# A two-block sequence model on one core: gate sigmoids placed ahead of other ScalarE steps, three output units run chunk by chunk, norm sums and one Toeplitz table product moved

## What is computed

```python
# odd mixer: 12 heads of 128 channels
p = h @ w_in                        # 1024 -> 1536 (xr) and 1536 (gate); h is RMS-normed
xc = causal_depthwise_conv(xr, conv_w, conv_b)       # 4 taps
r = sigmoid(xh @ w_rg + b_rg);  i = sigmoid(xh @ w_ig + b_ig)   # per head, 128x128 each
log_a = -8 * r * softplus(-lam);  a = exp(log_a)
bterm = sqrt(-expm1(2*log_a)) * (i * xc)
hs = associative_scan(a, bterm)     # along the sequence
h = h + (hs * silu(gate)) @ w_out
# block two, first mixer: a complex state space model, 64 groups of 16 channels, 64 states,
# then g = gelu(y + d*u), and out = (g @ w)[:, :1024] * sigmoid((g @ w)[:, 1024:])
```

## Time and profile before

| | us |
|---|---|
| median of 3 runs | 1717.25 |
| lowest and highest | 1715.61, 1717.97 |
| the profiled execution, its own time | 1717.2 |
| its span, first to last instruction | 1715.1 |
| PE busy | 1691.4 (99% of the span) |
| DVE, ACT, POOL busy | 871.1, 763.2, 967.1 |

### The profile page before, as it was taken

One profiled execution on the slowest core, in us unless ns is written; L12 is line 12 of the kernel. 1 busy time (PEld: TensorE's weight loads), 2 busy tenths in 40 slices (PEclk: granted clock), 3 DMA queues, 4 the chain that ended last, 5 costly groups with the idle time before them and its releaser, 6 DMA issues.

```text
span 1715.1 us, 20931 instructions
## 1 busy us (share of the span) xinstructions
PE 1691.4 (99%) x8044; PEld 1396.4 (81%) x8044; DVE 871.1 (51%) x1251; ACT 763.2 (44%) x1203; POOL 967.1 (56%) x606
## 2 busy tenths in 40 slices
PE   9999999999999999999999999999999999999998
PEld 7888888777778997888888888888678888888887
DVE  4999997757787885522212121386644221212124
ACT  5223335377867763343222222454765332323234
POOL 5859655657678575654444444664547444444464
PEclk9999999999999999999999999999999999999999
DMA  5322323222245233222222222222112222222221
GB/s 177 100 97 87 123 98 112 98 73 87 86 183 201 68 124 130 99 96 92 95 98 98 99 98 99 86 98 99 50 48 89 98 99 98 99 92 94 97 99 62
DMA packets 56258, 172.65 MB, mean 101 GB/s; under 512 B 6496, under 2 KB 14816, under 8 KB 55264
## 3 DMA queue, kind: packets, MB, share of 16 engines
q1 hardware_dynamic: 56160, 171.33, 28.9%
HBM read 165.01 MB, written 6.29 MB: 100 GB/s over the span
## 4 chain that ended last, share of the span: by engine, by line
PE 70%; DVE 5%; ACT 3%; issue 2%; POOL 1%; DMA 1%; SPq 0%; DVEq 0%; ACTq 0%
PE B L319 57%; PE B L1712 1%; PE B L2464 1%; PE B L2466 1%; PE B L2462 1%; PE B L2260 1%; PE B L2360 1%; PE B L2339 1%; DVE SW L1175 1%; PE B L302 1%; DVE B L1041 1%; PE B L1639 1%; PE B L1604 1%; PE B L304 1%; PE B L303 1%
## 5 line engine op out<-in xcount | busy, mean ns | idle before, releaser
L295 POOL TENSOR_TENSOR WL<-RAW,WH 128x1024 fp32r<-128x1024 f32 x280 | 679.0, 2427 | 618.3 <-ACT WH L291 618.0
L291 ACT ACTIVATE WH<-RAW 128x1024 fp32r<-128x1024 f32 x281 | 296.8, 1058 | 634.3 <-PE B L319 600.2
L319 PE MATMUL B<-P0h,WH 128*128 128x512 f32 x1088 | 424.6, 390 | 2.0 <-DVE Yl L444 1.8
L319 PE MATMUL B<-P0l,WH 128*128 128x512 f32 x1088 | 418.0, 389 | 0.3 <-DVE P0l L448 0.3
L319 PE MATMUL B<-P0h,WL 128*128 128x512 f32 x1088 | 274.4, 389 | 0.0
L319 PEld LDWEIGHTS B<-P0h,WH 128*128 128x128 f32 x1088 | 204.3, 188 | 45.8 <-DVE Yl L444 2.6
L319 PEld LDWEIGHTS B<-P0l,WH 128*128 128x128 f32 x1088 | 204.3, 188 | 42.8 <-DVE P0l L448 0.8
L319 PEld LDWEIGHTS B<-P0h,WL 128*128 128x128 f32 x1088 | 204.2, 188 | 42.4
L455 DVE TENSOR_TENSOR H<-H,B 128x512 f32<-128x512 f32 x88 | 60.2, 686 | 288.2 <-PE B L319 288.1
L1992 DVE SCALAR_TENSOR_TENSOR TMP<-B,RS 128x512 f32<-128x512 f32 x64 | 44.1, 691 | 258.5 <-PE B L319 244.1
L319 PE MATMUL B<-P1h,WH 128*128 128x512 f32 x448 | 174.7, 390 | 0.0
(11 more groups left out here) (362 smaller groups left out, 2686.5 us busy)
## 6 DMA issues: line engine op xcount, KB each, us to landing
RAW<-in_w SPq DMA_DIRECT2D x281, 512.0 KB, 3.2
PX<-in_zeros SPq DMA_DIRECT2D x4, 1024.0 KB, 9.4
H<-in_xT SPq DMA_DIRECT2D x8, 256.0 KB, 5.4
U<-u SPq DMA_DIRECT2D x32, 64.0 KB, 2.0
g<-GB SPq DMA_DIRECT2D x8, 256.0 KB, 2.2
GB<-g SPq DMA_DIRECT2D x32, 64.0 KB, 2.0
out<-Q SPq DMA_DIRECT2D x4, 512.0 KB, 3.6
CA<-in_zeros SPq DMA_DIRECT2D x1, 1920.0 KB, 10.0
```

The lines of the kernel that those rows point to most:

```text
L291: act.activation(WH[:, i % NS, :], RAW[:, i % NR, :], ACT.Copy).then_inc(*inc("w_hi", i))
L295: eng.tensor_tensor(WL[:, i % NS, :], RAW[:, i % NR, :], WH[:, i % NS, :].bitcast(F32), ALU.subtract).then_inc(*inc(lo_of(i), i))
L319: return pe.matmul(b[:, :], w[:, ws[c]], x[:, c, :], start=start, stop=stop)
```

## The change

In the odd mixer, ACT's work in slot X10 is only the weight copy; the first tap of X10 and the high part of X9 go into slot R1, between the sigmoids of heads 4 and 5 and those of heads 6 and 7, and the first tap of X11 and the high part of X10 behind the sigmoids of head 7. DVE's low part of X9 goes behind the scaling of X11. The one-column sigmoid stands after X8 in place of X9. The norm sums go from behind X0 into X1, behind its second chunk. In the state space stage, the table product of step 2 goes from behind `pe_v(2)` to ahead of `pe_y(0)`. The three output units run chunks 3 to 7 with the chunk outside and the unit inside.

```diff
             if kind in "XG":
-                linear(pe, what, P0h, P0l, range(8), ("x_lo", ("xc" if kind == "X" else "y", c)), "odd" if n == 0 else None)
+                linear(pe, what, P0h, P0l, range(8), ("x_lo", ("xc" if kind == "X" else "y", c)), "odd" if n == 0 else None,
+                       {1: lambda: stat_sums(pe, "odd", pool=rbanks)} if n == 1 else {})
...
-            if (kind, c) == ("X", 0):
-                stat_sums(pe, "odd", pool=rbanks)
-            elif (kind, c) == ("X", 1):
+            if (kind, c) == ("X", 1):
                 stat_spread(pe, "odd", pool=rbanks)
...
+    def held(n):
+
+        return 0 <= n < len(ODD) - 2 and ODD[n + 2] == ("R", 1)
...
-            if kind == "R":
+            if held(n):
+                highs(act, IDX[what] + 4)
+            elif kind == "R":
                 act_gates(act, pair(c, 0))
-                act_parts(act, n - 1)
-                if kind_at(n - 1) == "X":
+                if held(n - 2):
+                    act_first(act, n - 2)
+                    act_parts(act, n - 2)
+                else:
+                    act_parts(act, n - 1)
+                    if kind_at(n - 1) == "X":
+                        act_first(act, n - 1)
+                act_gates(act, pair(c, 1))
+                if held(n - 2):
                     act_first(act, n - 1)
-                act_gates(act, pair(c, 1))
-                if kind_at(n - 1) == "G":
+                    act_parts(act, n - 1)
+                elif kind_at(n - 1) == "G":
                     act_first(act, n - 1)
                 highs(act, IDX[what] + 3)
                 act_parts(act, n)
...
-            elif kind_at(n + 1) != "R":
+            elif kind_at(n + 1) != "R" and not held(n):
                 act_parts(act, n)
...
-            elif (kind, c) in (("X", 2), ("X", 9), ("G", 5)):
+            elif (kind, c) in (("X", 2), ("X", 8), ("G", 5)):
...
                     scaled(dve, XP[:, h % 2, 3:], ("in_odd", 0, h), "odd").then_inc(*inc("xp", h))
+                dve_parts(dve, n - 1, held(n - 1))
...
-            for unit, h in parted(n):
-                split_lo(dve, "xc" if unit == "X" else "y", h, Yl[:, h, :], own_bank(unit, h), Yh[:, h, :])
+            dve_parts(dve, n, not held(n))
...
+    def dve_parts(dve, n, due):
+        for unit, h in parted(n) if due else []:
+            split_lo(dve, "xc" if unit == "X" else "y", h, Yl[:, h, :], own_bank(unit, h), Yh[:, h, :])
...
         pe_transposes(pe, 3)
+        pe_toeplitz(pe, 2)
         for q in range(8):
             if q == 7:
                 banks.queue.extend(vbanks.queue)
-                pe_glu_start(pe, range(3))
+                pe_glu_start(pe)
             pe_y(pe, q)
             if q + 2 < 8:
                 pe_v(pe, q + 2)
-                pe_toeplitz(pe, q + 2)
+                if q:
+                    pe_toeplitz(pe, q + 2)
             if q + 4 < 8:
                 pe_transposes(pe, q + 4)
-        pe_glu_start(pe, range(3, 7))
         banks.queue.extend(ybanks.queue)
...
+    def pe_glu_start(pe):
 
         for what in GLU[:3]:
+            _, before = banks.take(what, "evac_a" if what[2] > 7 else "evac_d")
+            pe.wait_ge(*at(*before))
+            pe.wait_ge(*at("w_lo", IDX[what]))
+            for c in range(3):
+                pe_glu_chunk(pe, what, c)
+
+    def pe_glu_chunk(pe, what, c):
+
+        wh, wl = weights(IDX[what])
+        pe.wait_ge(*at("g_lo7" if c == 7 else "g_lo", ("g", c)))
+        ws = slice(128 * c, 128 * c + 128)
+        last = mm3(pe, banks.bank[what][:, :], wh[:, ws], wl[:, ws], P0h[:, c, :], P0l[:, c, :], c == 0, c == 7)
+        if c == 7:
+            last.then_inc(*inc("unit", what))
 
     def pe_glu(pe):
-        pe_glu_start(pe, range(7, 8))
+        for c in range(3, 8):
+            for what in GLU[:3]:
+                pe_glu_chunk(pe, what, c)
```

More of the change, by code:

```diff
@@ L1827, in program @@
     GLU = [("glu", 0, n + 8 * (1 - g)) for n in range(8) for g in range(2)]
-    def pe_glu_start(pe, chunks):
+    def pe_glu_start(pe):
         for what in GLU[:3]:
[L1832 to L1844, removed]
+            _, before = banks.take(what, "evac_a" if what[2] > 7 else "evac_d")
[10 more added lines that the diff above has]
+            last.then_inc(*inc("unit", what))
     def pe_glu(pe):
-        pe_glu_start(pe, range(7, 8))
+        for c in range(3, 8):
+            for what in GLU[:3]:
+                pe_glu_chunk(pe, what, c)
         for what in GLU[3:]:
```

## The result

The changed kernel takes **1722.67 us**, median of 9 runs (1720.76 to 1723.40), against 1717.25 (1715.61 to 1720.01) for the kernel before, 9 runs too: slower by 5.4 us by the medians. The ratio of all runs is 1.0027 [1.0019, 1.0036], or 4.6 us with an interval of 3.3 to 6.2, so the difference is clear of noise, but its size is known only to about 1.5 us. Forecast were 1721.9, range 1718.6 to 1724.3. The profiled execution took 1722.67 us with a span of 1720.6, where the kernel before had 1715.1, so the two traces differ by 5.5 us.

What follows compares the result with a forecast made beforehand. PE was taken as the bound, busy 99% of the span at full clock. On 1717.2 us, -0.9 + 0.6 + 5.1 + 2.5 - 2.6 = +4.7 gave 1721.9, range 1718.6 to 1724.3.

Steps and rivals of the forecast that it cites:

- norm sums: Sums moved behind two chunks of X1: the matmuls ahead fill 0.71 us of PE idle time; gain 0.9 us.
- gate steps: Odd mixer: R1 2.03 us shorter, but late taps delay y0's low part, G4 and G10; net loss 0.6 us.
- wait for the bank: Ahead of y(0): moved product waits for the copy of table product 1 until 582.7; loss 5.1 us.
- low clock: After the 6.9 us idle stretch, product and y(0) start at half clock; loss 2.5 us, bounds 1.7 to 4.4.
- output units: First three output units, chunk outside: the wait at chunk 6 goes; gain 2.6 us, bounds 2.3 to 2.7.
- Rival (c): Moved product's bank is free by 576, no wait, clock stays full: 1713.9, or 1711.3 with R1's gain; chance 0.05.
- Rival (a): Clock does not fall in the wait ahead of the product, all else as forecast: 1719.4 us; chance 0.12.
- rival (d): Low clock lasts 8.8 us, or the taps' chain passes on all its delay: 1723.8 to 1724.7; chance 0.09.
- Rival (b): Chain behind X9 to X11 has slack, so R1's gain of 2.0 us arrives: 1719.3 us; chance 0.12.

Runs made afterwards that it cites:

- third experiment: Kernel before with only the reordered gate steps of heads 4 to 7 and X9 to X11; 1717.82 us, ratio 1.0004.
- ninth experiment: Changed kernel with finer gate order and two-column sums spread in eights, table product of step 2 still ahead of y(0); 1717.73 us, ratio 0.9999.
- tenth experiment: Same kernel as the ninth experiment, plus 29 matmuls of 128x128 with unused results in the wait ahead of the table product; 1715.58 us, ratio 0.9991.
- the free bank: Changed kernel with the heads of two bank rings swapped, so the moved table product takes v(0)'s bank; 1715.14 us, ratio 0.9985.
- seventh experiment: Changed kernel with the table product back behind v(2) and sigmoids, high parts and first taps alternating more finely; 1712.35 us, ratio 0.9965.
- first experiment: Changed kernel with the table product of step 2 back behind v(2), all else kept; 1714.73 us, ratio 0.9988.

## Why the prediction was right, step by step

| step | forecast, us | measured, us |
|---|---|---|
| norm sums | -0.9 | -0.94, starts in the two traces |
| gate steps | +0.6 | +0.43 in the traces; +0.6 in the third experiment's median |
| wait for the bank | +5.1 | +5.3, ninth and tenth experiment |
| low clock | +2.5 | +2.15 there; 2.25 in the changed kernel's trace |
| output units | -2.6 | -1.5 over executions; -2.5 in the changed kernel's trace |
| sum | +4.7 | +5.4 (-0.94, +0.43, +5.3, +2.15, -1.5) |

**The wait for the bank.** It took place as worked out from the list of bank takes: nothing is taken between transposes 3 and the product, so it gets the bank of table product 1. The copy that the forecast saw end at 582.7 ended at 583.3, later by just the 0.6 us by which the transposes ahead of the wait were late too. The forecast's 5.1 us, the stall less the product's own time and less some of the waits behind it, is what arrived. The first matmul behind the last y shows it, at 655.65 in the changed kernel and in the kernel before at

```profile
647.64 0.47 PE L302 MATMUL B<-P0h,WH 128*128 128x512 f32 x1
```

From the last transposes ahead of the loop that is 80.29 us against 72.90, 7.39 more, and less the 2.25 of the low clock 5.14. The waits for the inputs U moved with it (1.1 us in all in the changed kernel, 1.2 before). Rival (c) hung on a copy done by 577, and was wrong in that. What (c) would have paid was too much even so: the free bank shows that the 1.46 us ahead of y(0) are not worth 0.45, since v(3) waits for its input next.

**The low clock.** 2.25 us come from two rows: the product takes 3.55 us from start to start and not 1.87, 1.68 more, and y(0) 5.10 instead of 4.53, 0.57 more. Rival (a) is out by the 0.50 of the clock's row, rival (d) by its length: the clock is at full again just after 588, some 4.6 us behind the restart, of which half is lost. Its other condition, that the taps' chain passes on all its delay, was not met either, as G10 shows below. The size, 2.5 from bounds of 1.7 to 4.4, was a choice within what the earlier trace rows allow. It came out near, but the runs do not show it to be one number: 2.25 and 1.4 us in two traces, 2.15 over the executions. Nor is the idle time ahead of the fall, put at about 5 us: in the ninth experiment's trace PE is idle from 571.5, and by the 0.60 of 574 to 577 the clock fell near 574.6. The rows are also weaker than the forecast took them: it read the low clock at the kernel's start from the distances of matmuls, while the profile's own column shows 1.00 there:

```profile
5.00:10.00 5.00, 4.20 (x15) 3.52 (x15) 4.17 (x6) 3.96 (x6) 0.00 (x0) 1.00 1.02 363
```

**The gate steps.** R1 took 7.42 us for 7.43 forecast, and G4 waited as forecast, for y0's low part. The last matmul of X0, ahead of all that was changed, started at 335.61 and at 336.10 before, so 0.5 us of any gain in the trace is scatter. Without it G4 is 1.2 us earlier (436.39 for 438.13), where the forecast had 1.1 (0.2 for the gates and the sums' 0.9), and G10 is 0.5 us earlier (478.05 for 479.05), where it had 0.3 (0.9 less 0.6). From -0.5 at G10 and -0.94 for the sums comes the +0.43 of the table. Rival (b), that R1's whole gain arrives, is refuted by 1.48 us of wait at G4. The seventh experiment shows the reason from the other side: with the taps not late, the gain arrives and more.

**The norm sums.** Eight matmuls at 336.88, with 0.2 us of wait in place of 0.7. This part was not tried by itself; its number is from the traces alone. It may be worth more over executions: the clock fell at these sums in two of the five traces that have them in their old place, behind 0.72 us of idle time, and in none of the seven that have them inside X1, where 0.2 us of idle time or none is left.

**The step that was mis-sized** is the output units. That the wait goes was right, and chunk 7 did not wait either. In the changed kernel's trace the three units take 10.62 us (655.65 to 666.27) where they took 13.12 (647.64 to 660.76), 2.5 less, as forecast. But 2.6 was read from one execution, and the wait differs between executions from 0.95 to 2.4 us; the gain over executions is about 1.5. The forecast's bounds, 2.3 to 2.7, did not hold it. That is 1.1 us too much gain; the low clock (0.35) and the gates (0.2) came out smaller than forecast, the wait for the bank 0.2 larger, and together this is the 0.7 us between +4.7 and +5.4. These errors partly cancel, which is luck; and 0.7 us is less than what the measurement of the whole can tell.

**What it did not see**: the clock's falls behind narrow matmuls. They cost 1.6 us each. The one behind the sixteen comes with either kernel, so over executions it should leave the difference as it is; the one at the norm sums may be rarer with the change. But the profile of before, with none in that place, gave no sign of them, and the one in the changed kernel's would have been put down to the gates had only the two traces been compared.

What stays open: why such a fall comes in one execution and not in the next of the same kernel; and where the 0.5 us lie between the first experiment's 1714.73 and what its parts give (-0.9, +0.4 and -1.5 make 1715.2), which is no more than one such fall moves a median (two in five executions spared the fall at the norm sums would be 0.6 us, an estimate from those traces). Nor was it tried why the spread sums keep the clock where sixteen in a row do not: their place in the sequence, their spacing and the idle time ahead of them changed together.

## What to carry to other kernels

A step that is moved ahead on an engine keeps its place in the ring of buffers: list the takes between the previous user and the new place, and look up when that user's copy ends, for what was idle time of 1.5 us becomes a wait of 7 us. Where PE's idle time grows to several microseconds, add what the low clock takes behind it, here 1.4 to 2.3 us on top of a wait that costs 5.3. And before gate or activation work is brought forward, follow what it pushes back: here fine alternation was 2.4 us faster than the block order, and the block order no faster than the old one.

## What the runs showed of the hardware

- The clock can fall while PE shows hardly any idle time: behind sixteen matmuls with two columns (1.9 us of them, 0.3 us idle ahead) it went to half for 3.4 us and cost 1.6 us in 5 of 9 traces, at eight with one column and 0.72 us idle ahead in 2 of 5. In the same nine traces it did not fall behind either of the two further rows of sixteen, which have no idle time ahead of them, nor in the 3 traces with the sums in eights among wide matmuls. The Trainium skill, "TensorE: Matmul & The Clock Gate", section on the clock gate, has the clock follow how busy the engine has been; by these rows the profile's busy share does not tell it: PE is shown busy for all of the stretch that the clock is low.
- Much of this kernel's scatter between executions goes with the mean clock, from 1715.8 to 1721.6 us, as the table shows. That such falls are what moves it is seen in the traces only, not in the timed executions. Comparing at equal mean clock parted 1.5 us from 2.6 here, where the ratios did not.
- Filling a 7 us wait with 29 matmuls of 128x128 in f32 (58 in the trace, 6.64 us) kept the clock at 1.00, in both traces that have it, and the product behind them takes 1.94 us and not 3.37 to 3.62.
- Behind the unfilled wait of 6.95 us the clock stayed at half for 4.6 us in the changed kernel's trace and for 3.0 in the ninth experiment's.
